# Weight preparation at the end of each FFN turn, and a split last pair of columns, beside the forgetting attention's weighted parts

## The reference

```python
def conv_ffn(h, w_up, conv_w, conv_b, w_down):
    u = h @ w_up                                  # 256x1024 @ 1024x5632
    u = lax.conv_general_dilated(u, conv_w[:, None, :], window_strides=(1,),
                                 padding=[(CONV_WIDTH - 1, 0)], ...) + conv_b   # 3 taps
    a, b = u[..., :D_FF], u[..., D_FF:]           # D_FF = 2816
    return (jax.nn.silu(a) * b) @ w_down
...
        x = x + jnp.concatenate([o_mix, o_mem], axis=-1) @ w_o[l]
        x = x + conv_ffn(rms_norm_2(x, ffn_norm[l]), w_up[l], conv_w[l], conv_b[l], w_down[l])
    return rms_norm_2(x, final_norm)
```

## Time and profile before

| | us |
|---|---|
| median of 3 runs (lowest, highest) | 1345.94 (1341.12, 1346.96) |
| profiled execution, its own time | 1349.2 |
| its span | 1347.2 |
| PE busy in the span | 1151.3 (85%) |
| DVE busy | 944.9 (70%) |
| ACT busy | 695.0 (52%) |
| POOL busy | 109.2 (8%) |
| mean granted TensorE clock | 0.914 of full speed |

### The profile page before, as it was taken

One profiled execution on the slowest core, in us unless ns is written; L12 is line 12 of the kernel. 1 busy time (PEld: TensorE's weight loads), 2 busy tenths in 40 slices (PEclk: granted clock), 3 DMA queues, 4 the chain that ended last, 5 costly groups with the idle time before them and its releaser, 6 DMA issues.

```text
span 1347.2 us, 24902 instructions
## 1 busy us (share of the span) xinstructions
PE 1151.3 (85%) x10399; PEld 1071.6 (80%) x10399; DVE 944.9 (70%) x1725; ACT 695.0 (52%) x1252; POOL 109.2 (8%) x114
## 2 busy tenths in 40 slices
PE   6799876979799659859976699999999769999986
PEld 6788765978688649748864599998999749999886
DVE  5687954666878755676768767788667575778852
ACT  5643256556432465555436656655644464565551
POOL 2000000110000011151000010111000001011100
PEclk9899986989899968969977899999899979999988
DMA  8232110344232104315340054454555304454450
GB/s 332 101 121 96 65 63 1 133 149 155 94 122 71 58 1 172 120 60 219 138 144 1 1 188 144 170 180 158 198 180 193 125 1 140 146 185 161 172 184 32
DMA packets 24447, 167.54 MB, mean 124 GB/s; under 512 B 2704, under 2 KB 2832, under 8 KB 8208
## 3 DMA queue, kind: packets, MB, share of 16 engines
q1 hardware_dynamic: 24336, 165.96, 35.2%
HBM read 164.90 MB, written 1.05 MB: 123 GB/s over the span
## 4 chain that ended last, share of the span: by engine, by line
PE 42%; DVE 34%; ACT 16%; issue 5%; DMA 1%; POOL 1%; POOLq 0%; DVEq 0%; SPq 0%; ACTq 0%
DVE WL L381 8%; PE ps L427 8%; PE ps L422 7%; PE ps L424 7%; DVE ARENA L2051 5%; ACT WH L368 4%; DVE FR L381 4%; PE ps L445 3%; PE ps L453 3%; PE ps L447 3%; ACT ARENA L745 2%; ACT FR L368 2%; PE ps L643 2%; DVE ARENA L2043 2%; ACT L484 2%
## 5 line engine op out<-in xcount | busy, mean ns | idle before, releaser
L381 DVE TENSOR_TENSOR WL<-raw,WH 128x1024 fp32r<-128x1024 f32 (+4 forms) x225 | 262.3, 1189 | 134.0 <-ACT WH L368 133.6
L422 PE MATMUL ps<-FR,WH 128*128 128x256 f32 x1248 | 310.6, 288 | 25.3 <-ACT WH L368 20.4
L424 PE MATMUL ps<-FR,WH 128*128 128x256 f32 x1248 | 306.5, 285 | 1.2 <-DVE FR L493 0.8
L368 ACT ACTIVATE WH<-raw 128x1024 fp32r<-128x1024 f32 (+4 forms) x225 | 217.0, 988 | 109.8 <-PE ps L427 63.5
L422 PEld LDWEIGHTS ps<-FR,WH 128*128 128x128 f32 x1248 | 244.5, 196 | 30.7 <-ACT WH L368 17.7
L424 PEld LDWEIGHTS ps<-FR,WH 128*128 128x128 f32 x1248 | 244.4, 196 | 3.3 <-DVE FR L493 1.9
L422 PE MATMUL ps<-FR,FR 128*128 128x256 f32 x680 | 170.9, 288 | 6.6 <-ACT FR L368 5.9
L427 PE MATMUL ps<-FR,WL 128*128 128x256 f32 x1248 | 171.8, 281 | 0.3 <-DVE WL L381 0.3
L424 PE MATMUL ps<-FR,FR 128*128 128x256 f32 x680 | 169.5, 286 | 0.2 <-DVE FR L493 0.2
L381 DVE TENSOR_TENSOR FR<-raw,FR 128x1024 fp32r<-128x1024 f32 (+2 forms) x100 | 117.2, 1194 | 65.5 <-ACT FR L368 65.5
L427 PEld LDWEIGHTS ps<-FR,WL 128*128 128x128 f32 x1248 | 158.0, 192 | 0.6 <-DVE WL L381 0.6
(11 more groups left out here) (313 smaller groups left out, 1774.5 us busy)
## 6 DMA issues: line engine op xcount, KB each, us to landing
raw<-wst_in SPq DMA_DIRECT2D x124, 1024.0 KB, 5.0
raw<-wst_in SPq DMA_DIRECT2D x14, 768.0 KB, 4.4
raw<-wst_in SPq DMA_DIRECT2D x11, 896.0 KB, 6.0
raw<-wst_in SPq DMA_DIRECT2D x4, 968.0 KB, 4.7
raw<-wst_in SPq DMA_DIRECT2D x2, 912.0 KB, 4.6
cst<-cst_in SPq DMA_DIRECT2D x1, 1681.0 KB, 15.4
X<-xT_in SPq DMA_DIRECT2D x2, 512.0 KB, 6.4
ARENA<-memT_in SPq DMA_DIRECT2D x1, 1024.0 KB, 4.8
```

The lines of the kernel that those rows point to most:

```text
L368: a.activation(hi[:, 0:cols], src, ACT.Copy).then_inc(*put("split_hi", ("hi", i)))
L381: v.tensor_tensor(lo[:, 0:cols], src, hi[:, 0:cols].bitcast(F32), SUB).then_inc(*put("split_lo", ("lo", i)))
L422: pe.matmul(out, hv[:, k, :], src.hi[:, c, :], start=k0 == 0 and k == ks[0], stop=False)
L424: pe.matmul(out, hv[:, k, :], src.lo[:, c, :], start=False, stop=False)
```

## The change

Four edits are in it. (1) In the FFN's loop the preparation of items for turn i + 1 stands at the end of turn i; on ACT one of the two items of a turn (`ahead` one smaller) stands between the centre taps and `part_hi`, the other at the end. (2) The three turns without new chunks prepare too: events `("up", l, 22)` to `("up", l, 25)` are set behind the first spans of w_down. (3) In FFN 1 the last pair of columns gets two banks; the mean of chunks 0 to 5 is started between two items of the last column, and chunks 6 and 7 are squared alone and added by PE. (4) ACT multiplies every chunk of X by the final norm's weight ahead (XG), so that the end has four products of 128x512, and the result is stored in four pieces. The rest of the kernel, with the parts `HK` and `HX` that FFN 0 makes for the forgetting attention (`fox_hi`, `fox_lo`), stays as it is.

```diff
@@ ffn_pe
             for c in range(4):
                 feat("w_down_2", l, r(128 * c, 128 * c + 128), m.F, ("F", l), first[c][:, 0:256], "down1", l, c, kc=FC, span=span)
+                if span[0] == 0:
+                    B.at_items["up", l, FC + c] = len(B.plan)
         for c0 in range(4, 8, 2):
+            if l == 1 and c0 == 6:
+                last_pe()
+                break
...
+    XG = Map(TOP2 - 2 * KC * S)(KC * S, "p (c t) -> p c t", c=KC)
+
+    def last_pe():
+        m, mean = fm[1], mean_bank[:, 0:S]
+        for c in (6, 7):
+            ps = begin_bank("last", c)
+            for span in ((0, 8), (8, FC)):
+                feat("w_down_2", 1, r(128 * c, 128 * c + 128), m.F, ("F", 1), ps[:, 0:256], "last", c, kc=FC, span=span)
+                if (c, span[0]) == (7, 0):
+                    qpe.wait_ge(*got("summed", ("f", 1), 4))
+                    qpe.wait_ge(*got("mean free", B.mean_before))
+                    for x in range(2):
+                        pe.matmul(mean, C("mean"), m.sq[0][:, x, :], start=x == 0, stop=False)
+        for c in (6, 7):
+            qpe.wait_ge(*got("square", ("f", 1), c))
+            ins = pe.matmul(mean, C("mean"), m.sq[3][:, c - 6, :], start=False, stop=c == 7)
+        ins.then_inc(*put("mean", ("mean", ("f", 1))))
+
+    def last_v(v, q):
+        for c in (6, 7):
+            split_lo(v, q, "last", c)
...
+            v.tensor_tensor(X[:, c, :], X[:, c, :], ps[:, 0:256], ADD).then_inc(*put("ffn_v", ("x f", 1, c), free))
+
+    def weigh_a(a, c):
+        a.activation(XG[:, c, :], X[:, c, :], ACT.Copy, scale=vcol("final_norm_2", None, c)).then_inc(*put("part_hi", ("xg", c)))
+
+    def last_a(a, q):
+        m = fm[1]
+        for c in (6, 7):
+            split_hi(a, q, "last", c)
+            q.wait_ge(*got("x f", 1, c))
+            q.wait_ge(*got("summed", ("f", 1), 2))
+            a.activation(m.sq[3][:, c - 6, :], X[:, c, :], ACT.Square).then_inc(*put("square", ("square", ("f", 1), c)))
+            weigh_a(a, c)
@@ ffn_v
             if i < FC:
-                split_lo(v, q, "up", l, i)
                 if i == 0:
+                    split_lo(v, q, "up", l, i)
...
                 part_lo(v, q, "part_lo_v", m.F, ("F", l), n, m.fb[n % 3])
+            split_lo(v, q, "up", l, min(i + 1, FC + 3))
@@ ffn_a
             if i < FC:
-                split_hi(a, q, "up", l, i)
                 if i == 0:
+                    split_hi(a, q, "up", l, i)
...
+            split_hi(a, q, "up", l, min(i + 1, FC + 3), ahead=NW + NMORE - 2)
             if 0 <= i - 2 < FC:
...
                 a.activation(u, u, ACT.Silu).then_inc(*put("ffn_a", ("silu", l, n)))
+            split_hi(a, q, "up", l, min(i + 1, FC + 3))
         table(a, LNEXP)
...
+            if l == 1:
+                weigh_a(a, c0)
+                weigh_a(a, c0 + 1)
@@ ffn_g
-        sum_squares(g_, q, ("f", l), fm[l].sq)
+        sum_squares(g_, q, ("f", l), fm[l].sq, (1, 2, 3) if l == 0 else (1, 2))
@@ SP, at the end
-        for h in range(2):
-            q.wait_ge(*got("out x", 4 * h + 3))
-            eng.dma_start(chunks(out_d)[:, 4 * h:4 * h + 4, :], X[:, 4 * h:4 * h + 4, :]).then_inc(*land("store"))
+        for c in range(0, KC, 2):
+            q.wait_ge(*got("out x", c))
+            eng.dma_start(chunks(out_d)[:, c:c + 2, :], X[:, c:c + 2, :]).then_inc(*land("store"))
@@ DVE, at the end
-        for c in range(KC):
-            v.scalar_tensor_tensor(X[:, c, :], X[:, c, :], vcol("final_norm_2", None, c), mean_bank[:, 0:S], MUL, MUL) \
-                .then_inc(*put("scaled", ("out x", c)))
+        for c in range(0, KC, 2):
+            q.wait_ge(*got("xg", c + 1))
+            v.tensor_tensor(X[:, c:c + 2, :], XG[:, c:c + 2, :], bc(mean_bank[:, 0:S], 1, 2), MUL).then_inc(*put("scaled", ("out x", c)))
```

More of the change, by code:

```diff
@@ L2014, in ffn_pe @@
         B.mark("PE", "end", ("F", l), "PE")
+    XG = Map(TOP2 - 2 * KC * S)(KC * S, "p (c t) -> p c t", c=KC)
[17 more added lines that the diff above has]
+            split_lo(v, q, "last", c)
+            ps, free = psum("last", c)
+            q.wait_ge(*got("last", c))
+            v.tensor_tensor(X[:, c, :], X[:, c, :], ps[:, 0:256], ADD).then_inc(*put("ffn_v", ("x f", 1, c), free))
[9 more added lines that the diff above has]
+            weigh_a(a, c)
     FOX_IN = ("HK", "HX"), (("kv_norm_2", None), ("attn_norm_2", 1))
@@ L2066, in ffn_v @@
                 continue
+            if l == 1 and c0 == 6:
+                last_v(v, q)
+                break
             split_lo(v, q, "down", l, c0)
@@ L2099, in ffn_a @@
                 a.activation(u, u, ACT.Silu).then_inc(*put("ffn_a", ("silu", l, n)))
+            split_hi(a, q, "up", l, min(i + 1, FC + 3))
         table(a, LNEXP)
         for c0 in range(0, 8, 2):
+            if l == 1 and c0 == 6:
+                last_a(a, q)
+                break
             if c0 < 4:
@@ L2712, in _ @@
         ffn_pe(1)
-        mean_mm(("f", 1), fm[1].sq[0])
     @block.vector
```

## The result

The changed kernel takes 1331.09 us (median of 4 runs, 1329.96 to 1332.38) against 1343.53 us for the kernel before (median of 4, 1340.12 to 1346.96). The ratio is 0.9906 with a 95% interval of 0.9881 to 0.9932: about 12.6 us gained (9.1 to 16.0) where 24.7 were forecast, outside the range 1315.5 to 1329.0. The profiled execution has a span of 1328.2 us (before 1347.2).

What follows compares the result with a forecast made beforehand. PE was taken to run out of prepared weight items because DVE and ACT need 6.10 us per chunk against its 5.60. Savings of 21.5 in the FFNs and 3.2 at the end, 24.7 us, gave 1321.2 us, range 1315.5 to 1329.

Steps and rivals of the forecast that it cites:

- Sum 5.56 us: FFN loop: predicted time per chunk of the DVE and ACT preparation after the change, against 5.60 us for PE.
- the 21.5 us for the FFNs: Both FFNs: predicted saving, 8.2 and 8.5 us of PE time plus 2.4 us of half clock each.
- The prediction's own sign of being wrong: FFN loop: a DVE and ACT time above 5.95 us per chunk would show the forecast wrong.
- Another of its signs: FFN loop: DVE's idle before L381 was to fall from 1.10 us to below 0.7.
- the lead: FFN loop: PE's five items prepared ahead, losing 0.50 us per chunk before the change; predicted to shrink no longer.
- the margin: FFN loop: a time per chunk up to some 5.95 us would make no hole in PE within 22 chunks.
- The circle: FFN loop: chain L2043, centre taps, rounding, F part, SiLU, rounding, residual, back to L2043; 5.56 us per chunk predicted.
- residual to L2043 1.14: FFN loop: time on DVE from a residual's start to L2043's, taken as half of 861.88 to 864.16.
- DVE's own 5.00 lies below: FFN loop: DVE's work without its 1.10 us idle is 5.00 us per chunk, so it would not set the pace.
- the slack: FFN tail: the last F part ready at about 13 us, needed by PE at 22.4; 9 us to spare, waits costed at nothing.
- Rival D: FFN tail: F parts over 9 us later than counted stop PE at w_down's second span; 28.5 us slower, 1374.4, chance 0.03.
- Rival A: FFN loop: middle rounding delays SiLU as much as it spares, 6.10 us stays; gain 19.3, 1326.6 us, chance 0.08.

## Why the prediction was wrong

What PE waits for, where filling the tail pays and what sets the end were right; the term of the loop failed, "Sum 5.56 us" with PE setting the cadence. The loop took 6.25 us. Of the 21.5 us for the FFNs came 5.9 + 6.2, 9.4 less; against the kernels with a loop of 5.93 or less the changed kernel loses 4.4 + 4.8. The prediction's own sign of being wrong is there, a loop above 5.95. Another of its signs is met for the wrong reason: DVE doesn't idle before L381 any more, but it idles 0.72 us before L501 instead.

- **PE's 2.80 us per item, the lead, the margin: right.** With a cadence of 5.93 or less the 48 items take 134.9 and 134.5 us, which is 2.80 to 2.81 each. With 6.05 PE loses 0.4 and 0.9 us, with 6.25 4.4 and 4.8. With 6.10 and both roundings behind SiLU it loses 3.0 and 3.5: where the roundings stand counts beside the cadence.
- **"Sum 5.56 us": wrong by an edge.** The circle ran through ACT to SiLU and on. It left out that DVE's `part_lo` stands ahead of the residuals in DVE's list and waits for ACT's `part_hi`, which the change moved behind a rounding. I had seen that move, but counted `part_hi` on ACT only, and asked about the queue behind the waiting rounding in the tail, not in the loop. The true circle is centre taps, rounding, `part_hi`, `part_lo`, two residuals: 0.72 + 1.00 + 0.95 + 0.43 + 0.34 + 2.28 = 5.72. Alone this would have cost nothing: 5.72 is below 5.95, and the runs with the product elsewhere show 5.72 and no hole.
- **GpSimd: no term at all in the loop.** The product took 0.75 us and was no bound, and the prediction gives no reason for leaving it out. It had run in DVE's idle 1.10 us, and the change fills that idle time. Then the two exclude each other, 0.54 us more for the residuals on the circle, 5.72 + 0.54 = 6.26. In the forecast's terms it is "residual to L2043 1.14", taken from a loop without the product beside it: from the second residual's start to L2087 it is now 1.68. That is the decisive miss: with the product away from the residuals the kernel gains what was forecast or a little more (ratio 0.9797, 27 us, 25 to 29).
- **"DVE's own 5.00 lies below": right as a sum, useless as a cover.** It took durations from a loop in which DVE and GpSimd never met.
- **Tail: the gain right, the slack wrong.** 8.6 and 7.9 us per FFN by the run without it, against 8.1 (5.7 and 2.4) in the forecast (the item at half clock took 4.94 us in FFN 0, 946.34 to 951.28, so 2.1 there), and ACT's waits in its queue cost PE nothing. But the F part of the last chunk was to be there 13 us after PE's last up item, and came after 24.3 (924.25 to 948.51). The count had ACT's queue and not DVE, whose L2087 for that chunk starts at 937.25 only. PE's second span begins at 948.44, before the part is there; it costs nothing only because this chunk is the last of the span's six and is used 1.2 us later. In the kernel with the product beside the taps 7.2 us are left (940.09 to 947.31). Rival D was nearer than its argument says; that it stayed away in the changed kernel is in part luck.
- **End: right in each piece,** Ln at 1.66 us, products 2.48, 9.4 in all, 0.9 paid ahead for 1.0. The store's 0.3 is 0.4.
- **Rival A** was the nearest, "the cadence stays 6.10": it has the loop that doesn't shorten and the tail that is filled. Its reason was false: SiLU does come later, 2.97 us after L2087 where it was 2.42, but it is not on the circle. Its gain of 19.3 us is still well above the 12.6 that came. The case that happened, a cadence above the old one, was not among the rivals.

## What to carry to other kernels

When an edit fills an engine's idle time, look up what the other engines do in exactly that time; a small operation off the critical path may have lived there and collide. When an instruction is moved in one engine's list, follow every later instruction of that list to who waits for it, and sum the circle again through each of them. And a queue of prepared items forgives a cadence that is a little too slow, so the number to reach is not equality but the point at which the lead lasts to the end.

## What the runs showed of the hardware

In these runs DVE and GpSimd exclude each other for whole instructions when DVE's operation reads two tensors from SBUF. A product of GpSimd alone takes 0.75 us. Issued 0.01 us after a residual of DVE it takes 1.81: read as 1.06 of waiting and 0.75 of work, in which the next residual stands for 0.54. Issued in the middle of one it takes 1.47, and the next residual loses 0.43. Beside taps of 0.4 us each it takes 0.82, and the taps lose 0.48. Beside the one operation tried with an operand in PSUM neither loses anything (0.74 and 0.68). Doubled, it costs DVE nothing more, since the second product waits for the residual and then runs beside that operation. The Trainium skill (SBUF — State Buffer, section SBUF: two separate sides) states this as an exclusive lock on a shared pair of ports, held for a whole instruction; a DVE operation with two SBUF inputs against a GpSimd operation that reads SBUF is one of its cases. By that rule, the trace agrees in all five places, and the product beside the residual should have been a term of the forecast.
